# Expert stage of a fused block: experts in pairs, four column groups, 96 places, plain fp32

## What is computed

```python
N_EXPERTS, TOP_K, D_EXPERT = 32, 4, 1024              # 512 tokens, D_MODEL = 1024

def clamped_swiglu(gu):
    gate, up = gu[..., :D_EXPERT], gu[..., D_EXPERT:]
    gate = jnp.minimum(gate, 7.0)
    up = jnp.clip(up, -7.0, 7.0)
    return (up + 1.0) * gate * jax.nn.sigmoid(1.702 * gate)

logits = xt @ w_router + b_router                      # top 4 of 32 experts per token
...
hb = clamped_swiglu(xb @ w_gu[e] + b_gu[e])            # xb: the tokens of expert e
yb = hb @ w_down[e] + b_down[e]                        # times the token's gate, added up
```

## Time and profile before

| | us |
|---|---|
| median of 3 runs | 2788.36 |
| the runs | 2793.61, 2788.17, 2788.36 |
| span of the profiled execution | 2788.0 |
| expert stage in it, first to last matmul of L1207 and L1230 | 1157.3 |
| one turn of its loop | 35.6 |

### The profile page before, as it was taken

How to read it: one execution, slowest core, us unless ns; L and a number is a source line. 1 busy time by engine, 2 the same in 40 slices (tenths; PEclk the granted TensorE clock), 3 DMA queues, 4 the chain that set the end, 5 groups by cost and what they waited for, 6 DMA issues and landing times. The chain is left out here.

```text
span 2788.0 us, 41851 instructions
## 1 busy us (share of the span) xinstructions
PE 2607.5 (94%) x16642; PEld 2086.0 (75%) x16642; DVE 1847.9 (66%) x1789; ACT 1466.4 (53%) x1628; POOL 630.1 (23%) x243
## 2 busy tenths in 40 slices
PE   8989987999999999999999989979988699899998
PEld 6668755788888888888888757757677577788887
DVE  6575246899999999999999943546745433422233
ACT  4344334677777777777777742336645322522222
POOL 0003002244444444444444320001132000000000
PEclk9989998999999999999999989989999899999999
DMA  5344224899999999999999853431000323122220
GB/s 209 120 157 138 85 89 181 332 383 382 382 382 381 384 382 383 382 382 382 382 383 382 352 210 128 152 109 68 20 33 4 119 87 134 48 98 99 91 100 36
DMA packets 114571, 595.70 MB, mean 214 GB/s; under 512 B 12144, under 2 KB 13936, under 8 KB 69808
## 3 DMA queue, kind: packets, MB, share of 16 engines
q1 hardware_dynamic: 98944, 539.07, 49.7%
q0 software_dynamic: 7056, 25.69, 3.0%
q10 hardware_dynamic: 8448, 29.17, 2.7%
HBM read 568.72 MB, written 25.17 MB: 213 GB/s over the span
## 5 line engine op out<-in xcount | busy, mean ns | idle before, releaser
L1352 DVE TENSOR_TENSOR weights_low<-weight_ring,weights_high 128x2048 fp32r<-128x2048 f32 x384 | 865.1, 2284 | 56.0 <-ACT weights_high L1298 55.8
L1298 ACT CAST weights_high<-weight_ring 128x2048 fp32r<-128x2048 f32 x384 | 726.8, 1909 | 180.9 <-PE psum L1207 146.9
L1167 POOL TENSOR_SCALAR rank_onehot<-iota,members 128x128 bf16<-128x128 f32 x132 | 442.0, 3358 | 1.0 <-issue 0.2
L358 DVE TENSOR_TENSOR w_low<-weight_ring,w_high 128x2048 fp32r<-128x2048 f32 (+1 forms) x92 | 213.7, 2324 | 326.0 <-ACT w_high L353 325.7
L353 ACT CAST w_high<-weight_ring 128x2048 fp32r<-128x2048 f32 (+1 forms) x88 | 166.6, 1893 | 291.6 <-PE psum L392 146.3
L1207 PE MATMUL psum<-weights_high,expert_x_high 128*128 128x512 f32 x1024 | 279.0, 394 | 2.9 <-DVE expert_x_low L1356 2.9
L1207 PE MATMUL psum<-weights_low,expert_x_high 128*128 128x512 f32 x1024 | 274.7, 390 | 0.0
L1207 PE MATMUL psum<-weights_high,expert_x_low 128*128 128x512 f32 x1024 | 274.5, 390 | 0.0
L1161 POOL DMA_INDIRECT expert_x<-hidden,index x33 | 89.7, 2718 | 776.4 <-DVE index L1347 593.6
L1207 PEld LDWEIGHTS psum<-weights_low,expert_x_high 128*128 128x128 f32 x1024 | 193.0, 189 | 40.5
L1207 PEld LDWEIGHTS psum<-weights_high,expert_x_low 128*128 128x128 f32 x1024 | 192.8, 188 | 40.2
(11 more groups left out here) (549 smaller groups left out, 4515.4 us busy)
## 6 DMA issues: line engine op xcount, KB each, us to landing
weight_ring<-in_w_gu SPq DMA_DIRECT2D x256, 1024.0 KB, 8.9
weight_ring<-in_w_down SPq DMA_DIRECT2D x128, 1024.0 KB, 8.9
weight_ring<-in_w_in SPq DMA_DIRECT2D x35, 1024.0 KB, 4.8
weight_ring<-in_w_ada SPq DMA_DIRECT2D x24, 1024.0 KB, 4.9
weight_ring<-in_w_ffn_in SPq DMA_DIRECT2D x22, 1024.0 KB, 4.9
expert_table<-expert_y ACTq DMA_DIRECT2D x32, 512.0 KB, 9.2
weight_ring<-in_w_ffn_out SPq DMA_DIRECT2D x11, 1024.0 KB, 4.9
weight_ring<-in_w_out SPq DMA_DIRECT2D x8, 1024.0 KB, 5.6
```

What stands on the lines that cost most here:

```text
L358: self.m.nc.vector.tensor_tensor(low, w, high.bitcast(F32), ALU.subtract).then_inc(self.ready.sem, 1)
L1167: last = nc.gpsimd.tensor_scalar(oc[:, t, :], iota[:, :], members[:, t, e], None, ALU.is_equal)
L1298: nc.scalar.copy(high[:, n % 4, :], slot(n)).then_inc(rounded.sem, 1)
L1352: V.tensor_tensor(low[:, n % 4, :], slot(n), high[:, n % 4, :].bitcast(F32), ALU.subtract).then_inc(ready.sem, 1)
```

## The change

- Experts go in 16 pairs. One expert has 96 places instead of 128, three row blocks of 32 (`CAP = NR * ROUND`). Tokens beyond would again take the flagged second pass.
- Nothing is split. The products are plain fp32. The stationary operand is 32 columns, one row block of one expert; four products, for two experts and two halves of 512 columns, go to the four column groups of TensorE, that is to partitions 0 to 31, 32 to 63, 64 to 95 and 96 to 127 of one bank. So a bank holds one row block, and partitions hold (expert, half of the columns). Gate takes banks 0 to 2, up banks 3 to 5, down banks 0 to 2 again; banks 6 and 7 serve lists and turnings.
- A pair has 16 slots of w_gu and 8 of w_down. w_down is loaded as whole rows of 8 KB per partition (two rows of the matrix) instead of two pieces of 4 KB; `turn_h` picks every second column to match.
- The ring's six slots are joined by six of `more_weights` for this stage: twelve. A slot is freed by TensorE (`ring.used`), two at a time.
- ScalarE copies x and h after the turnings and takes the sigmoids; VectorE takes the gates, the clamped product per row block, the copy of the result, and the one-hots, for two experts in one instruction (`mark_group`). GpSimd only gathers.
- The result is stored by four DMAs per pair, with rows of 2 KB.
- In `project_and_route` the first list is made for two experts; `moe_exit`'s second pass is adapted to 96 places.

The core of the diff, with most removed lines left out:

```diff
-CAP = 128
+EG = 2
+ROUND = 32
+NR = 3
+CAP = NR * ROUND
...
+GROUPS = E // EG
+EXTRA = 6
...
+def gate_up_units(dram, e):
+    return [dram["w_gu"][e(i), k * P:(k + 1) * P, :] for k in range(GUN) for i in range(EG)]
+def down_units(dram, e):
+    return [dram["w_down"][e(i), q * 2 * P:(q + 1) * 2 * P, :] for q in range(DNN) for i in range(EG)]
+def gate_up_rows(z):
+    return z.rearrange("a p n -> p (a n)") if len(z.shape) == 3 else z
+def down_rows(z):
+    return z.rearrange("a (p r) n -> p (a r n)", r=2) if len(z.shape) == 3 else z.rearrange("(p r) n -> p (r n)", r=2)
+def mark_group(nc, oc, iota, members, e):
+    return nc.vector.tensor_tensor(oc[:, :, :, :], iota[:, 0:CAP].unsqueeze(1).unsqueeze(1).to_broadcast([P, NT, EG, CAP]),
+                                   members[:, :, e].unsqueeze(3).to_broadcast([P, NT, EG, CAP]), ALU.is_equal)
...
+    x = [sb(f"expert_x{i}", [CAP, D]) for i in range(EG)]
+    xT, hT = sb("expert_xT", [P, KD, EG, CAP]), sb("expert_hT", [P, 4, NR, P])
+    g, u, s, y = (sb(n, [P, NR, 512]) for n in ("gate", "up", "sigmoid", "expert_y"))
+    more = sb("more_weights", [P, EXTRA, SLOT])
...
+    def slot(n):
+        i = n % SLOTS
+        return ring.buf[:, (U0 + i) % NSLOT, :] if i < NSLOT else more[:, i - NSLOT, :]
...
+            def load(n, src, late=0):
+                if n >= SLOTS:
+                    sp.wait_ge(ring.used, late + U0 + n - SLOTS + 1)
+                elif n < NSLOT:
+                    sp.wait_ge(ring.used, U0 + n - NSLOT + 1)
+                sp.dma_start(slot(n), src).then_inc(landing(n)[0], 16)
...
-            def mark_ranks(e):
-                for t in range(NT):
-                    last = nc.gpsimd.tensor_scalar(oc[:, t, :], iota[:, :], members[:, t, e], None, ALU.is_equal)
...
+            def turn_x(n, group):
+                i, c = n // 2, n % 2
+                if c == 0:
+                    pe.wait_ge(gathered[i].sem, group * 16 + gathered[i].at(16))
+                if n >= 2:
+                    pe.wait_ge(x_copied.sem, group * 4 + x_copied.at(n - 1))
+                for k in range(4):
+                    last = T.transpose(ps[6 + c][:, k * CAP:(k + 1) * CAP], x[i][:, (4 * c + k) * P:(4 * c + k + 1) * P], m.ident[0:CAP, 0:CAP])
                 last.then_inc(x_turned.sem, 1)
+            def turn_h(j, group):
+                pe.wait_ge(h_ready.sem, group * NR + h_ready.at(j + 1))
+                if j == 2:
+                    pe.wait_ge(h_copied.sem, group * NR + h_copied.at(1))
+                for b in range(4):
+                    o = b // 2 * 2 * P + b % 2
+                    last = T.transpose(ps[7 - j % 2][:, b * P:(b + 1) * P], u[:, j, o:o + 2 * P - 1:2], m.ident[:, :])
...
+            def list_rows():
+                for i in range(EG):
+                    for t in range(NT):
+                        last = T.matmul(ps[6][0:CAP, 2 * i:2 * i + 2], oc[:, t, i, :], tok[:, 2 * t:2 * t + 2], start=(t == 0), stop=(t == NT - 1))
...
+            def gate_up(n0, group, e=None, hook=lambda k: None):
                 for k in range(GUN):
+                    w = landed(n0 + 2 * k, e)
+                    hook(k)
+                    if k == 0:
+                        pe.wait_ge(x_copied.sem, group * 4 + x_copied.at(4))
+                    if k == GUN - 1:
+                        pe.wait_ge(sel_ready.sem, group + sel_ready.at(1))
+                    for o, (up, j) in enumerate((v, j) for v in ((0, 1) if k == GUN - 1 else (1, 0)) for j in range(NR)):
+                        if k == 0:
+                            if up:
+                                if e is not None:
+                                    pe.wait_ge(up_freed.sem, (e - 1) * NR + up_freed.at(j + 1))
+                            elif e is not None:
+                                pe.wait_ge(y_copied.sem, (e - 1) * NR + (y_copied.at(j + 1) - NR))
+                                pe.wait_ge(gate_ready.sem, (e - 1) * NR + gate_ready.at(j + 1))
+                        for q in range(4):
+                            i, c = q // 2, q % 2
+                            ins = T.matmul(ps[NR * up + j][quarter(q), :], xT[:, k, i, quarter(j)],
+                                           w[i][:, up * D + c * 512:up * D + (c + 1) * 512], start=(k == 0), stop=False)
+                            if o == 0 and q == 0:
+                                ins.then_inc(ring.used, 1 if n0 == 0 and k == 0 else 2)
+                        if k == GUN - 1:
+                            for q in range(4):
+                                i, c = q // 2, q % 2
+                                ins = T.matmul(ps[NR * up + j][quarter(q), :], sel[:, i, :],
+                                               bias[:, up * D + c * 512:up * D + (c + 1) * 512], start=False, stop=True)
+                            ins.then_inc((up_done if up else gate_done).sem, 1)
+            def down(n0, group, e=None, hook=lambda n: None):
+                for n in range(2 * DNN):
+                    q, r = n // 2, n % 2
+                    if r == 0:
+                        w = landed(n0 + 2 * q, e)
+                    hook(n)
+                    for j in range(NR):
+                        if n == 0:
+                            pe.wait_ge(h_copied.sem, group * NR + h_copied.at(j + 1))
+                            if e is not None:
+                                pe.wait_ge(gate_ready.sem, e * NR + gate_ready.at(j + 1))
+                            else:
+                                pe.wait_ge(y_copied.sem, y_copied.at(NR * LAST - NR + j + 1))
+                        for z in range(4):
+                            i, c = z // 2, z % 2
+                            ins = T.matmul(ps[j][quarter(z), :], hT[:, q % 2 * 2 + r, j, quarter(2 * i + q // 2)],
+                                           w[i][:, r * D + c * 512:r * D + (c + 1) * 512], start=(n == 0), stop=(n == 2 * DNN - 1))
+                            if r == 0 and j == 0 and z == 0:
+                                ins.then_inc(ring.used, 2)
+                        if n == 2 * DNN - 1:
+                            ins.then_inc(down_done.sem, 1)
...
+            def step(e, at_end=False):
+                def in_gate_up(k):
+                    if k == 1 and not at_end:
+                        pe.wait_ge(onehot.sem, e + onehot.at(1))
+                        list_rows()
+                    if 3 <= k < 3 + NR:
+                        if k == 4 and not at_end:
+                            pe.wait_ge(index_ready.sem, e + index_ready.at(1))
+                        turn_h(k - 3, e - 1)
+                def in_down(n):
+                    if 2 <= n < 6 and not at_end:
+                        if n < 4:
+                            pe.wait_ge(h_copied.sem, e * NR + h_copied.at(n - NR))
+                        turn_x(n - 2, e + 1)
+                gate_up(GU, e, e, in_gate_up)
+                down(GU + GU, e - 1, e, in_down)
...
-            def round_weights(n, e=None):
-                landed, used = 16 * (n // NSLOT + 1), n - 3
-                if e is not None:
-                    landed, used = (e - 1) * (16 * LOOP // NSLOT) + landed, (e - 1) * LOOP + used
-                act.wait_ge(ring.landed[n % NSLOT], landed)
-                act.wait_ge(ring.used, used)
-                nc.scalar.copy(high[:, n % 4, :], slot(n)).then_inc(rounded.sem, 1)
...
+            def y_out(group, e):
+                act.wait_ge(y_copied.sem, group * NR + y_copied.at(NR))
+                for z in range(4):
+                    i, c = z // 2, z % 2
+                    dst = table[e(i), :, c * 512:c * 512 + 512]
+                    dst = dst.rearrange("(j p) n -> p j n", p=ROUND) if len(dst.shape) == 2 else dst.rearrange("a (j p) n -> p (a j) n", p=ROUND)
+                    act.dma_start(dst, y[quarter(z), :, :]).then_inc(y_stored.sem, 16)
...
-            def rest_of_weights(n, e=None):
-                count = rounded.at(n - U0 + 1) if e is None else (e - 1) * LOOP + rounded.at(n - U0 + 1)
-                dve.wait_ge(rounded.sem, count)
-                V.tensor_tensor(low[:, n % 4, :], slot(n), high[:, n % 4, :].bitcast(F32), ALU.subtract).then_inc(ready.sem, 1)
...
+            def swiglu(group):
+                n = group * NR
+                for j in range(NR):
+                    dve.wait_ge(gate_done.sem, n + gate_done.at(j + 1))
+                    V.tensor_scalar(g[:, j, :], ps[j][:, :], 7.0, None, ALU.min).then_inc(gate_ready.sem, 1)
+                for j in range(NR):
+                    dve.wait_ge(up_done.sem, n + up_done.at(j + 1))
+                    V.tensor_scalar(u[:, j, :], ps[NR + j][:, :], 7.0, -7.0, ALU.min, ALU.max).then_inc(up_freed.sem, 1)
+                for j in range(NR):
+                    dve.wait_ge(sig_done.sem, n + sig_done.at(j + 1))
+                    V.tensor_tensor(g[:, j, :], g[:, j, :], s[:, j, :], ALU.mult).then_inc(gate_scaled.sem, 1)
+                for j in range(NR):
```

(30 more changed lines are left out.)

369 lines of the change are left out of this document (129 added, 240 removed).

## The result

The kernel after takes 2748.91 us in the median of four runs (2744.0 to 2752.93), against 2789.14 for the kernel before (2788.17 to 2793.61): a ratio of 0.9845, 95% interval 0.9818 to 0.9873. The forecast was 2737, range 2695 to 2790. The profiled execution has a span of 2742.2, 45.8 less than before.

What follows compares the result with a forecast made beforehand. TensorE was taken to bound the expert stage: 68.7 us a pair, the stage 1104 us, 53 less; minus 1.5 at the edges, rounded to 51. 2788.0 - 51 + 0.4 gives 2737 us, range 2695 to 2790.

Steps and rivals of the forecast that it cites:

- What bounds the pair: Expert stage: TensorE sets the pace at 68.7 us a pair, against 71.2 for two turns before; chance 0.55.
- The wave: Expert products: four matmuls at once in four column groups, 0.435 us a wave, 144 waves or 62.6 us a pair.
- The bursts of the modulation: Modulation products, same form at half the width: waves of four at 0.22 us, taken as the price for a long run.
- the range's far end, 0.50: Expert products: far upper end of 0.50 us a wave, 72 us a pair; slow rival's program 2887, its chance 0.13.
- The interruptions: TensorE leaves the column groups eight times per pair: 0.22 us each, 1.8 in all, bounds 0 to 4.
- DMA: Weight loads, gathers and table writes of a pair: 66.5 us, bounds 64.3 to 70, just below TensorE.
- the rival that the present rate of 383 GB/s would last: Expert stage: DMA becomes the bound, 69.8 us a pair, program 2755; chance 0.20 for the DMA-bound case.
- Code loaded each turn: Loop boundaries of the expert stage: code is loaded again at each of 15, 30 to 75 us, program 2780; chance 0.08.
- Row length: Loads of w_down: whole 8 KB rows were costed at nothing.
- VectorE's and ScalarE's share: Expert stage, per pair: VectorE busy 12 us and ScalarE 6 us of 68.7.
- Edges: Ends of the expert stage: cold start 3 us, exposed copies of x 1 and h 1, making the stage 1104.
- The last store: End of the expert stage: four issues instead of one, costing 0.8 us.

## Why the prediction was right, and where it was off

The prediction was right in what bounds the stage and in the price of its main part; it owes the closeness of its pair in part to luck, and it missed the exit.

- *What bounds the pair.* Right: TensorE, never idle, clock 1.00, and the loading queue waits for slots freed by it (564.2 us for L1261, 290.1 for L1288).
- *The wave.* 0.435 predicted, 0.430 measured: 61.9 us a pair for 62.6. The bursts of the modulation stood for a long run, and of the range's far end, 0.50, nothing showed. One group starts a matmul every 0.43 us, four groups four of them. The Trainium skill's 3.07 times for four row groups (TensorE: Matmul & The Clock Gate, Measured speedup vs the span model), from which the prediction estimated a wave of 0.557, is not borne out for these column groups, which reach four times the rate of one.
- *The interruptions.* Predicted 4.8 us with their transposes and the list (2.8 + 0.2 + 1.8), measured 3 x 0.81 + 4 x 0.61 + 0.56 (the list: 12 waves in 5.27 from 990.30 to 995.57, so 0.11, and 0.45 until 996.02) = 5.43. The price of an interruption was too low: 0.22 taken, 0.29 measured, within the bounds 0 to 0.5. With the bias at 1.3, as predicted, 61.9 + 1.3 + 5.43 = 68.63. The hit of 68.7 for 68.63 is thus in part luck: two errors, 0.7 and 0.6, cancel.
- *DMA.* 66.5 predicted, 64.9 measured as its floor; the rival that the present rate of 383 GB/s would last is out, and the table writes and gathers (313 and 344 GB/s beside them) make TensorE wait nowhere.
- *Code loaded each turn.* Out: no gap at any boundary, with 640 matmuls in a pair. A branch that costs 5 us is elsewhere, at the exit, and I had not looked there. What the Trainium skill says of a taken branch out of the window (Runtime: NRT & Kernel Launch, Instruction fetch mechanics) would fit it, but no row here shows what the branch waits for.
- *Row length, and VectorE's and ScalarE's share.* The rows made no load late, but the strided turn that they call for cost 0.27 a pair. 12 and 6 us were predicted, 11.15 and 5.56 measured.
- *Edges: the mis-sized term.* The stage was put at 1104 and took 1100.7 (16 x 68.63 is 1098.1; the cold start and the exposed copies cost 2.6 and not 5). The start was to be 0.7 later and was 2.2; in the experiments it lies anywhere from 457.2 to 467.6, the two ends in kernels in which nothing ahead of it was edited, so this term can't be told from the spread. The last store was to cost 0.8 and the exit cost 9.0. About 4.5 of it are the first wait: 2.6 went when the loads that a rule for six slots holds back were issued earlier, and the other 1.9, four issues in place of one among them, were not taken apart. The other 4.5 are the second wait, behind the long branch. Of the 11.9 us between 2737 and the median, 0.4 are the rounding of the sum, 5.2 this net (45.8 for 51), 1.4 lie around the span (1.8 in place of 0.4), and 4.9 are the distance of the profiled run, the fastest of its kernel at 2744.0, from the median. I had costed "the exit fetches as many rows as before" and not asked what is issued beside it.

Where the gain comes from can be read per place. For 512 columns and one row block of 128 the kernel before spent three products of 0.227, 0.68 us, on 128 places, 5.3 ns a place. Now a group of four products (two waves, 0.86 us) serves 32 places of two experts and two halves, so 96 places cost 3 x 0.86 / 4 = 0.645 us, 6.7 ns a place. Plain fp32 in four groups is dearer per place; it wins, by 5%, because 96 places are computed and not 128. This is arithmetic on the two traces; no run has the four groups with 128 places.

## What to carry to other kernels

Four column groups gave four times the rate of one here, with neighbours in the queue in different groups; with one group after the other most of that was lost. Count the interruptions, at 0.29 us each here beside their own work, and put them together. When a stage gets slots of its own, look at what the rules for the old ones now hold back at its end. Read a change of 1% from its stage, since the unchanged remainder moved by up to 14 us between the executions shown.

## What the hardware showed that I had not expected

- One group's matmuls follow each other at 0.43 us; at a change of group four of the next start beside the last four of the one before.
- A turn of h, four transposes, costs 0.68 us from every second column and 0.58 from neighbouring ones.
- The same 9164 matmuls behind the exit's start took 1162.6 to 1176.3 us, and the granted clock differs stretch by stretch: in the 40 us from 200 us behind the first exit product it was 0.97 in the profile of the kernel after and 0.80 to 0.82 in three of the experiments, in the next 40 us 0.90 and 0.87.
- Moving TensorE's code by 64 instructions took 4.7 us off one wait (7.31 to 2.60) and shortened the branch ahead of it from 5.63 to 0.45.
